# The first mixer of a four-layer kernel: weights loaded first, keys and values in one chunk, high products ahead of low ones, rotary products out of PSUM

## What is computed

```python
hn = rms_norm(h, norm_mix_g[layer])
proj = hn @ ab_w_in[j]
qa, ka, va, qb, kb, vb = jnp.split(proj, split_ab, axis=-1)
qa = rms_norm(qa.reshape(b, s, A_HEADS, HEAD_DIM), a_q_norm_g[j])      # 8 heads of 64
ka = rms_norm(ka.reshape(b, s, A_KV_HEADS, HEAD_DIM), a_k_norm_g[j])   # 2 heads of 64
qa = apply_rope(qa, cos_ax, sin_ax)
ka = apply_rope(ka, cos_ax, sin_ax)
o_a = gqa_attention(qa, ka, va.reshape(b, s, A_KV_HEADS, HEAD_DIM))
o_b = dilated_attention(qb, kb, vb, rel_bias)
mix = jnp.concatenate([o_a, o_b], axis=-1) @ ab_w_out[j]
```

## Time and profile before

| | |
|---|---|
| median of 3 runs | 1275.93 us (1275.86 to 1277.51) |
| profiled execution | 1281.55 us, span 1279.7 us |
| mean granted TensorE clock | 0.971 |
| busy: TensorE, GpSimd, ScalarE, VectorE | 1211.6, 955.8, 679.5, 623.2 us |
| chunks of weights | 186 |

### The profile page before, as it was taken

The page is one execution under the profiler, slowest core; times in us unless marked ns, Lnnn a source line. Parts: engine busy times, 40 slices in busy tenths (PEclk is TensorE's granted clock), DMA queues, the critical chain, the costliest instruction groups (busy, mean ns, idle before and its releaser), DMA issues.

```text
span 1279.7 us, 20261 instructions
## 1 busy us (share of the span) xinstructions
PE 1211.6 (95%) x7822; PEld 1081.0 (84%) x7822; DVE 623.2 (49%) x1076; ACT 679.5 (53%) x920; POOL 955.8 (75%) x750
## 2 busy tenths in 40 slices
PE   4899999999989999999999998999997898999997
PEld 4788998999968998999988777888886876888885
DVE  4866344210485244210542755777405646587712
ACT  5365655444565655444454346656546565656741
POOL 4846679978843779979795446899895854789985
PEclk9799999999999999999999898999998989999999
DMA  6562345554431446545553123555554442436551
GB/s 262 191 184 104 133 155 208 197 178 176 174 124 43 165 145 217 195 168 178 196 193 134 66 74 133 189 206 203 184 201 156 139 159 102 165 138 234 204 184 64
DMA packets 33132, 208.56 MB, mean 163 GB/s; under 512 B 3432, under 2 KB 7656, under 8 KB 8472
## 3 DMA queue, kind: packets, MB, share of 16 engines
q1 hardware_dynamic: 29728, 199.22, 43.6%
q10 hardware_dynamic: 3320, 8.14, 2.0%
HBM read 206.29 MB, written 1.59 MB: 162 GB/s over the span
## 4 chain that ended last, share of the span: by engine, by line
POOL 56%; issue 24%; PE 16%; DVE 2%; ACT 1%; DMA 0%; POOLq 0%; DVEq 0%; SPq 0%; ACTq 0%
POOL w_lo L2350 56%; PE bank L332 6%; PE bank L334 3%; PE bank L284 2%; PE bank L286 2%; PE bank L285 2%; ACT w_hi L1090 0%; DMA raw<-stream 0%; DVE stats L1681 0%; PE bank L1032 0%; ACT arena L1528 0%; ACT h L1188 0%; DVE bank L1695 0%; POOLq L2347 0%; PE bank L1047 0%
## 5 line engine op out<-in xcount | busy, mean ns | idle before, releaser
L2350 POOL TENSOR_TENSOR w_lo<-raw,w_hi 128x512 fp32r<-128x512 f32 x744 | 953.1, 1319 | 308.1 <-ACT w_hi L1090 307.9
L1090 ACT ACTIVATE w_hi<-raw 128x2048 fp32r<-128x2048 f32 x186 | 353.8, 1910 | 187.5 <-PE bank L286 110.0
L332 PE MATMUL bank<-xs,w_hi 128*128 128x512 f32 x1024 | 361.7, 398 | 3.1 <-DVE xs L1600 3.1
L334 PE MATMUL bank<-xs,w_lo 128*128 128x256 f32 x1024 | 287.3, 281 | 0.0
L332 PEld LDWEIGHTS bank<-xs,w_hi 128*128 128x128 f32 x1024 | 193.6, 189 | 50.4 <-issue 3.9
L284 PE MATMUL bank<-xs,w_hi 128*128 128x256 f32 x624 | 183.3, 294 | 20.6 <-POOL w_lo L2350 17.6
L284 PE MATMUL bank<-hT_hi,w_hi 128*128 128x256 f32 x680 | 194.7, 286 | 2.1 <-issue 1.9
L334 PEld LDWEIGHTS bank<-xs,w_lo 128*128 128x128 f32 x1024 | 194.5, 190 | 0.0
L286 PE MATMUL bank<-hT_hi,w_lo 128*128 128x256 f32 x680 | 192.4, 283 | 0.0
L285 PE MATMUL bank<-xs,w_hi 128*128 128x256 f32 x624 | 179.8, 288 | 0.0
L286 PE MATMUL bank<-xs,w_lo 128*128 128x256 f32 x624 | 179.4, 288 | 0.0
(11 more groups left out here) (318 smaller groups left out, 1600.5 us busy)
## 6 DMA issues: line engine op xcount, KB each, us to landing
raw<-stream SPq DMA_DIRECT2D x186, 1024.0 KB, 4.8
arena<-ln_rows ACTq DMA_DIRECT2D x4, 1024.0 KB, 4.9
arena<-vec_scratch ACTq DMA_DIRECT2D x8, 256.0 KB, 9.0
con<-consts SPq DMA_DIRECT2D x1, 1288.0 KB
h<-x SPq DMA_DIRECT2D x1, 1024.0 KB, 5.0
out<-h SPq DMA_DIRECT2D x4, 256.0 KB, 2.3
con<-pool_mat ACTq DMA_DIRECT2D x1, 768.0 KB, 8.1
vec_scratch<-vec_row ACTq DMA_DIRECT2D x1, 512.0 KB
```

The lines of the kernel that those rows point to most:

```text
L332: mm(o[j][:, :], hi[:, k, s], xs[:, k, :, :].rearrange("p a t -> p (a t)"), start=(k == tiles_in[0]), stop=False, skip_group_check=True)
L334: last = mm(o[j][:, 0:T], lo[:, k, s], xs_hi[:, k, :], start=False, stop=(k == tiles_in[-1]), skip_group_check=True)
L1090: af(w_hi[:, c % CUT].rearrange("p a b -> p (a b)"), raw[:, c % RAW, :], ACT.Copy)\
L2350: ins = nc.gpsimd.tensor_tensor(w_lo[:, slot_c].rearrange("p a b -> p (a b)")[:, part], raw[:, slot_r, part], w_hi[:, slot_c].rearrange("p ...
```

## The change

In neutral words: SP issues chunk 0 of the weights first, then the parameters, then x in two halves (semaphores `x0_loaded`, `x1_loaded`, `par_loaded`), then the base constants. TensorE begins with all products of chunk 0's high weights (`high_products`), pair by pair as `xs_hi` and then `xs_lo` come, and multiplies the low weights after them (`low_products`); the two query chunks are split in the same way. VectorE makes `xs_lo` in two steps: gain times x into PSUM (bank 3 to 6), then that minus `xs_hi`. The two key heads, single now, and the values share chunk 0, so the stream has 185 chunks. The values come out with tokens along the free axis and are transposed. Query heads are reordered so that every pair has one head of each key head. The raw projections are kept in `raws`, and the product with the cosine table reads PSUM directly (`cosine`); the product with the sine table and the sum are apart from it (`sine`). The root and reciprocal of the key's sums stay in PSUM.

```diff
-STREAM = [("ab_k", 1), ("ab_q", 2), ("va", 1), ("vb", 1), ("b_qk", 3), ...
+STREAM = [("ab_kv", 1), ("ab_q", 2), ("vb", 1), ("b_qk", 3), ...
...
+            def high_products(c, key, first):
+                pe.wait_ge(S("w_hi_ready"), c + 1)
+                o = claim(pe, key)
+                if first:
+                    for src, ready in ((xs_hi, "xs_hi"), (xs_lo, "xs_ready")):
+                        for k in range(8):
+                            if k % 2 == 0:
+                                pe.wait_ge(S(ready), k // 2 + 1)
+                            for j in range(2):
+                                mm(o[:, j * T:(j + 1) * T], w_hi[:, c % CUT, k, j * P:(j + 1) * P], src[:, k, :],
+                                   start=(src is xs_hi and k == 0 and j == 0), stop=False, skip_group_check=True)
...
+            def low_products(c, key):
+                _, lo = chunk(c)
...
-            dense("ab_k", 1, wait="n0", pairs=True)
-            dense("ab_q", 2, between=sums_and_bias)
-            hi, lo = chunk(START["va"])
+            high_products(START["ab_kv"], ("ab_kv", 0), True)
+            low_products(START["ab_kv"], ("ab_kv", 0))
+            high_products(START["ab_q"], ("ab_q", 0), False)
...
+            low_products(START["ab_q"], ("ab_q", 0))
+            high_products(START["ab_q"] + 1, ("ab_q", 1), False)
...
             o = claim(pe, "va")
             for t in range(TT):
-                for k in range(8):
-                    s = slice(t * P, (t + 1) * P)
-                    last = three(o[:, t * P:(t + 1) * P], xs_hi[:, k, s], xs_lo[:, k, s], hi[:, k, 0:P], lo[:, k, 0:P],
-                                 start=(k == 0), stop=(k == 7))
...
-            pe.wait_ge(S("qa_sq"), 1)
-            swapped(0)
-            swapped(1)
+                last = nc.tensor.transpose(o[:, t * P:(t + 1) * P], raws[:, 5, t * P:(t + 1) * P], eye)
+            filled(last, "va")
+            low_products(START["ab_q"] + 1, ("ab_q", 1))
...
+            square_pair(0, pair_of_h(0))
+            square_pair(1, pair_of_h(1))
             cut(1)
-            for n in range(4):
-                if n >= 2:
-                    act.wait_ge(S("squares_free"), n - 1)
-                square_pair(n, pair_of_h(n))
+            act.wait_ge(S("squares_free"), 1)
+            square_pair(2, pair_of_h(2))
             cut(2)
+            act.wait_ge(S("squares_free"), 2)
+            square_pair(3, pair_of_h(3))
...
             for n in range(4):
-                low_pair(n, h[:, 2 * n:2 * n + 2, :].rearrange("p a b -> p (a b)"), ("mix_g", 0))
+                dve.wait_ge(S(f"x{n // 2}_loaded"), 16)
+                o = bank[made[("x_gained", n)][0]]
+                for j in range(2):
+                    ins = v.tensor_scalar(o[:, j * T:(j + 1) * T], h[:, 2 * n + j, :], pc("mix_g", 2 * n + j), None, ALU.mult)
+                ins.then_inc(S("x_scaled"), 1)
+                dve.wait_ge(S("x_scaled"), n + 1)
+                rest(xs_lo[:, 2 * n:2 * n + 2, :], o[:, :].rearrange("p (a b) -> p a b", a=2),
+                     xs_hi[:, 2 * n:2 * n + 2, :]).then_inc(S("xs_ready"), 1)
...
-                link(v.tensor_tensor(pair_of(n), pair_of(n), over(c, 2), ALU.mult))
...
+            def cosine(n):
+                o = full(dve, ("ab_q", n))
+                v.tensor_copy(pair_of(n, raws).rearrange("p a b -> p (a b)"), o[:, :]).then_inc(S("qa_copied"), 1)
+                drained(v.tensor_tensor(pair_of(n), o[:, :].rearrange("p (a b) -> p a b", a=2), over(tabs[0], 2), ALU.mult), ("ab_q", n))
...
-            sp.dma_start(h[:, :, :], x).then_inc(S("x_loaded"), 16)
+            sp.dma_start(raw[:, 0, :], stream[0]).then_inc(S("raw0"), 16)
+            sp.dma_start(par[:, :], params).then_inc(S("par_loaded"), 16)
+            for n in range(2):
+                sp.dma_start(h[:, 4 * n:4 * n + 4, :], x[:, 4 * n:4 * n + 4, :]).then_inc(S(f"x{n}_loaded"), 16)
```

More of the change, by code:

```diff
@@ L266, in evacuated @@
             eng.wait_ge(S(f"bank{b}_drained"), n)
+        for n in range(4):
+            fills[3 + n] += 1
+            made[("x_gained", n)] = [3 + n, fills[3 + n], None, None]
         block = ctx.enter_context(nc.Block())
@@ L486, in keep_gate_banks @@
                 gate_free[name] = fills[6:8]
[L488 to L497, removed]
-                else:
[L499 to L502, removed]
+            def high_products(c, key, first):
[9 more added lines that the diff above has]
+                                   start=(src is xs_hi and k == 0 and j == 0), stop=False, skip_group_check=True)
+                else:
+                    for j in range(2):
+                        for k in range(8):
+                            for src in (xs_hi, xs_lo):
+                                mm(o[:, j * T:(j + 1) * T], w_hi[:, c % CUT, k, j * P:(j + 1) * P], src[:, k, :],
+                                   start=(src is xs_hi and k == 0 and j == 0), stop=False, skip_group_check=True)
@@ L504, in swapped @@
+            def low_products(c, key):
+                _, lo = chunk(c)
+                o = bank[made[key][0]]
+                for j in range(2):
+                    for k in range(8):
+                        last = mm(o[:, j * T:(j + 1) * T], lo[:, k, j * P:(j + 1) * P], xs_hi[:, k, :], start=False, stop=(k == 7),
+                                  skip_group_check=True)
+                used_up(last)
+                filled_by_chunk(key, c)
             def swapped(n):
                 o = claim(pe, ("qa_swap", n))
-                filled(mm(o[:, :], cc("perm", 128), qa[:, 2 * n:2 * n + 2, :].rearrange("p k t -> p (k t)"),
-                          start=True, stop=True), ("qa_swap", n))
@@ L542, in v_tile @@
                     filled_by_chunk(("vb", n), c)
+            pe.wait_ge(S("qa_copied"), 1)
+            swapped(0)
             v_tile(0, 0)
+            pe.wait_ge(S("qa_copied"), 2)
+            swapped(1)
+            pe.wait_ge(S("qa_sq"), 2)
+            o = claim(pe, "qa_sums")
+            for t in range(TT):
+                for n in range(4):
+                    last = mm(o[:, 4 * n + t:4 * n + t + 3:2], sq[:, n, t * P:(t + 1) * P], cc("blk", 128)[:, 0:128:64],
+                              start=True, stop=True)
+            filled(last, "qa_sums")
             v_tile(0, 1)
@@ L647, in ab_step @@
                 if p < 4:
-                    pair_scores("AB", p, lambda i: half(qa, i)[:, i // 2, :], lambda i: half(qa, i)[:, 4 + i // 4, :])
+                    pair_scores("AB", p, lambda i: half(qa, i)[:, i // 2, :], lambda i: half(qa, i)[:, 4, :])
                 elif p < 8:
@@ L1312, in _ @@
+            cut(START["ab_q"] + 1 + AHEAD)
             act.wait_ge(S("row_stored"), 16)
             act.dma_start(vec_scratch, vec_row.unsqueeze(1).to_broadcast([8, 32, 512])).then_inc(S("vec_stored"), 16)
-            chunks("va", 1)
             cut(START["vb"] + AHEAD)
@@ L1865, in _ @@
-            rope(2, tabs[2], tabs[3])
-            o = full(dve, ("ab_q", 1))
-            drained(v.tensor_copy(pair_of(1).rearrange("p a b -> p (a b)"), o[:, :]), ("ab_q", 1))
-            for i in range(2):
-                evacuated(dve, ("ab_q", i))
-            v.engine_nop().then_inc(S("qa_copied"), 1)
-            evacuated(dve, "ka_ssq")
-            link(v.reciprocal(k_std, k_std))
-            evacuated(dve, ("qa_swap", 2))
-            v.tensor_tensor(pair_of(2), pair_of(2), k_std, ALU.mult).then_inc(S("ka_ready"), 1)
+                link(v.tensor_tensor(o, o, over(tabs[1], 2), ALU.mult))
@@ new lines, in sine @@
+                evacuated(dve, ("ab_q", n))
+                drained(v.tensor_tensor(pair_of(n), pair_of(n), o, ALU.add), ("qa_swap", n))
+                evacuated(dve, ("qa_swap", n))
+                v.engine_nop().then_inc(S("qa_ready"), 1)
+            cosine(0)
+            o = full(dve, "ka_ssq")
+            v.scalar_tensor_tensor(o[:, 0:T], o[:, 0:T], 1.0 / 64, eps_s, ALU.mult, ALU.add).then_inc(S("ka_mean"), 1)
+            o = full(dve, ("qa_swap", 2))
+            link(v.tensor_tensor(o[:, 0:T], o[:, 0:T], tabs[3], ALU.mult))
```

106 lines of the change are left out of this document (59 added, 47 removed).

## The result

| us | before | changed |
|---|---|---|
| median of 7 runs each | 1275.86 | 1264.9 |
| lowest to highest | 1272.73 to 1277.6 | 1263.13 to 1271.32 |
| profiled execution, span | 1281.55, 1279.7 | 1264.52, 1262.7 |
| mean granted clock, profiled | 0.971 | 0.974 |

The ratio is 0.9919, with a 95% interval of 0.9891 to 0.9946: the kernel is 11.0 us faster. I had said 1252.9 with a range of 1246 to 1264, so the gain is half of what I forecast. Three numbers should make the reader stop: I forecast 23.0 us, between the two profiled executions lie 17.0, between the two medians 11.0.

The account below looks back on a forecast made before the run. The prediction took TensorE, not GpSimd, to set the pace and counted its first 65.80 us. Terms summed to -23.7, with +0.7 allowed -23.0, so 1275.93 became 1252.9 us, range 1246 to 1264.

Parts of the forecast that it names:

- I think that they have it, and take the same difference: Timed runs of the kernel before contain the 4.3 us stall and slow clock, so 23.0 comes off their median too.
- the timed runs have no stall: Rival: 10.2 of the 23 us before the scores are not there to win; gain 13, 1263 us; chance 0.10.
- The argument of the 5.6 us: The median lies 5.6 us below the profiled execution; without stall and slow clock it would lie over 10 lower.
- Scores to end: What comes earlier at the first scores (65.80 us before) should come earlier at the end too.
- Start, -8.3: At the first loads: TensorE starts at about 8.95 us instead of 17.27, 8.3 us earlier.
- New waits, +0.6, VectorE's choice: In chunk 0: VectorE's low parts add 0.6 us at 0.49 a multiplication, 8.2 at the upper bound of 1.40.
- Values, -4.9: At the values before the scores: 48 products go and two transposes come, saving 4.9 us.
- Stall, -4.3: At the swap of the queries: TensorE's wait goes, saving 4.3 us.
- clock, -5.9: Behind the swap wait: 42 records in 11.7 us at half clock would take half, saving 5.9 us.
- Covers: Work hidden behind TensorE: eight gathers delay the exponentials to 45.5 us; 0.7 allowed before the first transposes and beside GpSimd.
- GpSimd as the bound: Rival: only GpSimd's own line counts, its start and one chunk; gain 9, 1267 us; chance 0.04.
- Slower: Rival: eight attention normalizations on VectorE each wait 4.3 us for GpSimd, 34 in all, giving 1287; chance 0.03.

Follow-up runs that it names:

- before_psum_all: The kernel before, with the products with the cosine table and the key's root, reciprocal and last product in PSUM: 1274.31 us, ratio 0.9977.
- before_weights_first: The kernel before, with only chunk 0 and the parameters loaded first: 1275.95 us, ratio 0.999.
- sbuf_low: The changed kernel, with xs_lo made as before by one instruction with two SBUF operands: 1268.02 us, ratio 0.9937 to the kernel before.
- plus_48: The changed kernel, with 48 unneeded products of 128 columns added behind the transposes of the values: 1270.09 us, ratio 0.9946 to the kernel before.
- x_first: The changed kernel, with the old load order (x in halves, base constants and parameters ahead of chunk 0): 1271.84 us, ratio 0.9952 to the kernel before.

## Why the prediction was wrong

The picture of the kernel up to the scores was right, and so was nearly every term of the sum, against the execution from which it was subtracted. The step that failed is the last one before the rivals: **"I think that they have it, and take the same difference"**. The 10.2 us of stall and slow clock (-4.3 and -5.9) are real in the profiled execution and absent in the second one, which took 1277.27; taking every such instruction of the key and of the rotary step away (`before_psum_all`) moved the median by 0.9 us. So the median of the timed executions did not hold them. What happened is the rival "the timed runs have no stall", with 1263 and a chance of 0.10; measured were 1264.9.

- **The argument of the 5.6 us.** I took it that without the stall the median would lie over 10 below the profile. It lay 5.6 below and lacked the stall all the same, since other stretches differ by as much between executions. The second profile of before gained 9.8 us at the scores, still had 9.7 of them when the cut of the 139th chunk began (942.7 and 933.0), and ended only 4.2 lower (1275.5 against 1279.7). The clock by stretch in late layers shows where part of that went, first in the first profile of before, then in the second:

```profile
950.00:1090.00 140.00, 121.01 (x685) 102.53 (x684) 75.15 (x130) 81.06 (x111) 91.53 (x71) 0.92 0.40 142
```

```profile
945.00:1090.00 145.00, 126.45 (x700) 107.69 (x699) 76.14 (x132) 81.44 (x112) 91.81 (x71) 0.88 0.37 130
```

  The clock averages 0.88 there instead of 0.92, and 145 x 0.88 is about the work of 140 x 0.92: 5 us longer for the same. A gap between one profile and a median is not evidence for or against one stall of that size; the profile of a second execution is.
- **Scores to end.** I took it that what comes earlier at the scores comes earlier at the end. An equally profiled execution was to take 1258.5 and took 1264.52: 6.1 of the 23.1 us went between the scores and the end, as told below.
- **Start, -8.3.** 7.4 us in the profiled pair (17.27 to 9.90). The half of x landed 0.9 later than worked out. In the profiled execution of `before_weights_first` the earlier start is paid back at the swap, and its median shows no gain.
- **New waits, +0.6, VectorE's choice.** The lower bound was the right one: 0.44 for a multiplication of 128 x 256 into PSUM beside a busy GpSimd, and chunk 0 took 0.3 us longer than before (8.1 against 7.8). The Trainium skill's page "GPSIMD Engine Reference", section "Key points", says that GpSimd contends with VectorE's two-port modes and with two SBUF inputs. By that, taken for this tensor-scalar product, the sum would have been -16.1. For the product, whose destination is in PSUM, the trace shows no contention: 0.87 us for two, beside a busy GpSimd and beside an idle one. For two SBUF operands it agrees (1.15 to 12.46 us on 128 x 512). The upper bound of +8.2 was too high in any case: `sbuf_low`, whose instructions took 1014 ns on average, put the scores 2.5 later.
- **Values, -4.9.** `plus_48` gives 5.4 for 48 products, and the two transposes took 0.4.
- **Stall, -4.3, and clock, -5.9.** Right for the pair of profiles, wrong for the timed runs, as above.
- **Covers.** The exponentials start at 46.50, one us after the 45.5 worked out. The transposes follow without a wait (50.90 behind a product at 50.78); TensorE waits 0.89 behind them, in front of the first values (+0.7 predicted). What I missed is the longest case: six gathers held the queue for 11.95 us in one execution.
- **GpSimd as the bound** falls by `plus_48`. **Slower** did not come: in the profiled execution the longest wait between the scores and the end of the first attention is that of 0.89 us, though two-operand normalizations run there.

For the pair without a stall the account is 13.5 us at the scores, and 12.3 at the end of the span (1275.5 and 1263.2). About 1 goes in front of the first values and 3 more by the end of the second layer's attention, and about 3 come back later. The first pair loses the same in both places and 2 more at the very end. In the second layer's attention a longer stretch at half clock goes with the loss (0.66 between 340 and 350 in the changed kernel, 0.83 between 350 and 360 in the second profile of before). Why it is longer stays open, as does what comes back. The 11.0 of the medians lie below 12.3 by less than the interval is wide (6.9 to 13.9 us).

Open, too: what decides whether a two-operand instruction gets its turn within about one piece of GpSimd (1.15 to 1.6 us) or only when GpSimd pauses. All four long ones ended with GpSimd's run: those of 7.23, 9.10 and 12.46 us some 0.55 us behind its end, that of 4.92 us at its end. L1859 alone can't be blamed: with it gone, L1876 stalled in its place.

## What to carry to other kernels

Before a stall of a few us enters a sum, look for it in a second profile, and look whether the timed runs of before fall into two groups: nearly half of the gain that I forecast was one execution's bad luck. Beside a GpSimd that runs without pauses, give VectorE's instructions at most one operand in SBUF, with the other in PSUM or as a scalar of the partition, and do it for all of the stretch and not for one, or the stall moves on. DMA issues ahead of activations on the same queue can hold these up, as in the profile of `x_first`; moving them behind cost nothing here.

## What was not expected of the hardware

- A VectorE instruction with two SBUF operands took 4.92 us on 128 x 1 numbers, and 0.21 as the form with a scalar of the partition.
- Such an instruction can wait through ten pieces of GpSimd, 12.46 us, and end only with GpSimd's run.
- Issuing six small gathers from ScalarE's queue took 11.95 us in one execution where five took 3.85 in another; the compute instructions behind them waited as long.
- Two executions of one program differ by 9.8 us at the 56th microsecond and by 4.2 at the end.
